# Neighbouring inner channels on one partition: 8192-byte stretches in the experts' down loads, every second column in the transposes

## What is computed

```python
def swiglu(h, w1, w3, w2):
    a = jnp.einsum('bsd,df->bsf', h, w1)
    b = jnp.einsum('bsd,df->bsf', h, w3)
    return jnp.einsum('bsf,fd->bsd', jax.nn.silu(a) * b, w2)

for e in range(N_EXPERTS):                       # 8 experts
    out = out + gates[..., e:e + 1] * swiglu(h, w1[e], w3[e], w2[e])
```

## Time and profile before

| | |
|---|---|
| device time, median of 3 | 1605.03 us (1604.75 to 1606.97) |
| device time of the profiled execution | 1604.42 us |
| its span on the core | 1602.6 us |
| TensorE busy | 1583.4 us (99%) |
| TensorE's weight loads | 1396.0 us (87%), beside the matmuls |
| VectorE busy | 1287.5 us (80%) |
| ScalarE busy | 1042.5 us (65%) |
| read from HBM | 450.74 MB, 282 GB/s over the span |
| expert loads | 336 issues of 1024 KB, 5.4 us to landing (median) |

### The profile page before, as it was taken

One profiled execution on the slowest core, in us unless ns is written; L12 is line 12 of the kernel. 1 busy time (PEld: TensorE's weight loads), 2 busy tenths in 40 slices (PEclk: granted clock), 3 DMA queues, 4 the chain that ended last, 5 costly groups with the idle time before them and its releaser, 6 DMA issues.

```text
span 1602.6 us, 23576 instructions
## 1 busy us (share of the span) xinstructions
PE 1583.4 (99%) x9473; PEld 1396.0 (87%) x9473; DVE 1287.5 (80%) x1137; ACT 1042.5 (65%) x958; POOL 18.7 (1%) x19
## 2 busy tenths in 40 slices
PE   9999999999999999999999999999999999999998
PEld 8999999999999898788888888888888887888886
DVE  6895875445798677998987988897988986988986
ACT  6555554335546557777777776777777776677674
POOL 0000100000000010000000000000000000000000
PEclk9999999999999999999999999999999999999999
DMA  9544545555444456999998999998999998999994
GB/s 298 172 152 139 183 160 185 187 185 191 146 157 159 142 174 227 357 371 359 374 369 325 372 371 360 372 369 311 371 369 362 370 369 308 363 361 378 360 364 173
DMA packets 182503, 453.28 MB, mean 283 GB/s; under 512 B 7168, under 2 KB 81024, under 8 KB 182272
## 3 DMA queue, kind: packets, MB, share of 16 engines
q1 hardware_dynamic: 182400, 451.82, 77.5%
HBM read 450.74 MB, written 1.05 MB: 282 GB/s over the span
## 4 chain that ended last, share of the span: by engine, by line
PE 94%; DVE 3%; ACT 1%; issue 1%; DMA 1%; SPq 0%; ACTq 0%; DVEq 0%
PE bank L310 29%; PE bank L312 29%; PE bank L311 29%; DVE w_low L300 2%; PE bank L1665 2%; PE bank L1643 1%; PE bank L1686 1%; DMA raw<-w_in 1%; ACT w_high L296 1%; PE bank L1283 0%; PE bank L1392 0%; PE bank L1460 0%; PE bank L1343 0%; PE bank L1438 0%; DVE rinv L905 0%
## 5 line engine op out<-in xcount | busy, mean ns | idle before, releaser
L300 DVE TENSOR_TENSOR w_low<-raw,w_high 128x2048 fp32r<-128x2048 f32 x426 | 958.0, 2287 | 124.3 <-ACT w_high L296 124.0
L296 ACT ACTIVATE w_high<-raw 128x2048 fp32r<-128x2048 f32 x426 | 804.2, 1918 | 158.5 <-DMA raw<-exp_w 154.8
L310 PE MATMUL bank<-w_high,hg_high 128*128 128x512 f32 x896 | 352.8, 394 | 4.7 <-DVE w_low L300 3.2
L312 PE MATMUL bank<-w_high,hg_low 128*128 128x512 f32 x896 | 349.7, 390 | 0.0
L311 PE MATMUL bank<-w_low,hg_high 128*128 128x512 f32 x896 | 349.6, 390 | 0.0
L310 PE MATMUL bank<-h_high,w_high 128*128 128x256 f32 x1024 | 290.5, 284 | 0.0
L312 PE MATMUL bank<-h_high,w_low 128*128 128x256 f32 x1024 | 285.7, 279 | 0.0
L311 PE MATMUL bank<-h_low,w_high 128*128 128x256 f32 x1024 | 285.7, 279 | 0.0
L310 PEld LDWEIGHTS bank<-w_high,hg_high 128*128 128x128 f32 x896 | 168.5, 188 | 41.0 <-DVE w_low L300 3.3
L312 PEld LDWEIGHTS bank<-w_high,hg_low 128*128 128x128 f32 x896 | 168.6, 188 | 35.6
L311 PEld LDWEIGHTS bank<-w_low,hg_high 128*128 128x128 f32 x896 | 168.7, 188 | 34.0
(11 more groups left out here) (295 smaller groups left out, 1590.4 us busy)
## 6 DMA issues: line engine op xcount, KB each, us to landing
raw<-exp_w SPq DMA_DIRECT2D x336, 1024.0 KB, 5.4
raw<-w_in SPq DMA_DIRECT2D x41, 1024.0 KB, 5.0
raw<-ffn_w SPq DMA_DIRECT2D x33, 1024.0 KB, 5.1
raw<-w_out SPq DMA_DIRECT2D x8, 1024.0 KB, 4.8
raw<-w_br_attn SPq DMA_DIRECT2D x4, 1024.0 KB, 4.9
raw<-w_br_pool SPq DMA_DIRECT2D x2, 1024.0 KB, 5.2
raw<-w_br_conv SPq DMA_DIRECT2D x2, 1024.0 KB, 4.8
cst<-consts SPq DMA_DIRECT2D x1, 1280.0 KB, 14.1
```

Of the source, the lines that this page charges most:

```text
L296: nc.scalar.activation(wh[c % RING][:], raw[c % RING][:], ACT.Copy).then_inc(s["high_done"], 1)
L300: nc.vector.tensor_tensor(wl[c % RING][:], raw[c % RING][:], wh[c % RING][:].bitcast(F32), ALU.subtract).then_inc(s["split_done"], 1)
L310: pe.matmul(dst, lh, rh, start=start and i == 0, stop=False)
L312: last = pe.matmul(dst, ll, rh, start=False, stop=stop and i == len(terms) - 1)
```

## The change

Partition p of a down piece now takes the neighbouring channels 2p and 2p + 1 of the piece: one stretch of 8192 bytes. To match, block k of the transposes takes every second column (k, k + 2, ...) of 256 columns of `guE`.

```diff
-            e2 = exp_w2[0].rearrange("e (b k p) n -> e b p k n", p=P, k=2)
+            e2 = exp_w2[0].rearrange("e (b p k) n -> e b p k n", p=P, k=2)
...
                 def turn(count, a):
                     pe.wait_ge(s["m_mult"], count + a)
                     for k in range(4):
-                        ins = pe.transpose(bank[TURN_BANKS[a]][:, k * P:k * P + P],
-                                           guE[:, 512 * a + k * P:512 * a + k * P + P], ident)
+                        pairs = guE[:, 512 * a + 256 * (k // 2):512 * a + 256 * (k // 2) + 256].rearrange("p (c two) -> p two c", two=2)
+                        ins = pe.transpose(bank[TURN_BANKS[a]][:, k * P:k * P + P], pairs[:, k % 2, :], ident)
                     ins.then_inc(s["m_t"], 1)
```

## The result

The changed kernel takes 1607.82 us, the median of 20 runs (1604.73 to 1612.65); the kernel before 1604.23 us (20 runs, 1602.10 to 1607.79). The ratio is 1.0024, with a 95% interval from 1.0018 to 1.0031: it is slower by 0.24%, 3.6 us by the medians. (A ratio here is estimated over all executions and is not the quotient of the two medians; in the experiments the two differ by up to 1.3 us.) The time lies in the range that was forecast (1602 to 1611); the forecast of the likeliest case, no change within 0.2%, does not hold to the letter: the measured slowdown stands just beyond that bound, where 0.15 of the chance had been.

The account below looks back on a forecast made before the run. The prediction took TensorE to bound the kernel. From the profiled 1604.42 us, -0.1 for the loads and +0.5 for the transposes gave 1604.8, or 1605.4 us on the scale of the median of runs; range 1602 to 1611.

Parts of the forecast that it names:

- the likeliest case: Whole kernel: loads and transposes both within 1.1 us of nothing, so no change within 0.2%; chance 0.73.
- The bound: Experts' stretch: TensorE, busy 99%, sets the pace of the loads; a load has some 4 us of cover over.
- the 9 us of transfer time: Down loads: 0.08 us saved per piece, 9 us in all; almost none counts on TensorE's path, taken as -0.1 us.
- The packets: Kernel's load queue: 14336 packets fewer, 168064, and that many not under 8 KB beside the 231.
- Their price: Down loads: one packet of 8192 bytes replaces two of 4096 and saves 10 ns of 346, 3%.
- The transposes: 224 weight loads on TensorE, read from `guE` with a step of 8 bytes: +0.5 us in all.
- the near bound: Transposes' weight loads: 1024 bytes passed over at 9.0 bytes per ns, 5 ns more each, 1.1 us in all.
- The nearest row: TensorE's moving operand of 512 columns: 2048 bytes of each partition in 227 ns, 9.0 bytes per ns.
- The bound from above: Transposes' weight loads: each column fetched alone costs twice, 108 ns more each, +24.3 us in all.
- The signs listed for the forecast: New profile: transposes' weight load stays at 138 to 145 ns, four at 0.59 to 0.61 us, a turn at 0.43 us.
- The slower rival: Transposes: strided load halves the rate, load doubles, 1629 us; full chance 0.08, partial over 14 ns per transpose 0.07.
- The 0.80 for "same": Whole kernel: chance of no change, 0.73 for the forecast plus 0.07 for loads that don't become longer packets.

Follow-up runs that it names:

- the loads and the turns alone: Kernel before with only the down loads at 8192 bytes per partition: 1603.76 us, ratio 0.9997; with only the transposes at every second column: 1606.28 us, ratio 1.0018.
- the long row of strided transposes: Kernel before with each turn's transposes made five times over, taking every second column: 1715.05 us, against 1702.72 us for the same with packed transposes.
- the two later measurements: The whole change measured again, unaltered, beside the kernel before: 1608.65 us, ratio 1.0021, and then 1606.53 us, ratio 1.0019.
- the loads alone: Kernel before with only the down loads taking 8192 bytes per partition, transposes packed as before: 1603.76 us, ratio 0.9997.

## Why the prediction came out as it did

**The bound** was read rightly: TensorE sets the pace, and a load has cover. Of the 9 us of transfer time that were to be saved nothing arrives, in the traces (943.3 to 943.4 us against 943.5) or in the times (0.9997, 1.0002, 1.0000 in the three measurements with long packets, packed transposes and a multiply of 684 ns).

**The packets** came as worked out, 168064 and 14336 long ones. Their price came out as well: by the packets' own times in the trace of the changed kernel, from 650 us on, one of 8192 bytes takes 339 ns on average and one of 4096 bytes 175, so the long one saves 10 ns of two short ones, as worked out. In the share of the DMA engines the saving drowns: 78.0% against 77.5% before, and 77.9 and 78.3% with the loads and the turns alone. ScalarE's waits for loads, which might have shrunk by 9 us, did not in this trace (143.0 against 141.9); over the traces of all kernels in the table above they are 137.5 to 144.2 us with long packets and 141.9 to 151.6 without, so a few us may be saved there. None of it reaches TensorE.

**The transposes** are the step that failed in size: "take the middle of 0 and 1.1, +0.5 us". The term measured 224 x 10.4 ns = 2.3 us, twice the upper end of the near bound. The nearest row had been a moving operand that is read packed; it bounded how many bytes are passed over in a time, and said nothing of what a step costs. The bytes that a strided load passes over were the wrong measure, since a step twice as long costs nearly the same. The place was right: the moving operand and the output were left as they were, only the load was made strided, and TensorE paid for each of the 224. The bound from above held too, and so did the 108 ns per packed transpose, which gave 97 us for 896 more of them where 98.7 were measured. The signs listed for the forecast failed too: the load lasts 208 ns, not 138 to 145, and four of them 0.67 us, not 0.59 to 0.61. The slower rival, a load that costs twice, would have gone wrong as well: the load's duration rises by half while its cost on TensorE rises by a tenth (in the long row of strided transposes each load lasts 208 ns and they are 118 ns apart, so the loads overlap).

**The rule of the Trainium skill** ("SBUF — State Buffer", the note on SBUF cachelines). That two hits per line of 16 bytes run at the full rate would have put the sum at 0 for a step of 8 bytes, and a penalty at a step of 16. This case's trace agrees with neither: the load lasts 208 ns, and the transpose costs 10 ns more, at a step of 8; at 16 it is 210 ns and 11 ns more. The measurement decides.

**The rest.** The medians of the whole change stand 3.6, 4.2 and 2.6 us over before, with ratios 1.0024, 1.0021 and 1.0019; the turns explain 2.3 us, 1.0014. The last two intervals hold 1.0014, the first (from 1.0018) does not. The fastest execution of the change is 2.6, 2.4 and 1.8 us above the fastest of the kernel before, near the 2.3, and the table above has 2.9 in its middle. What the medians have beyond that is likely a matter of how often TensorE's clock falls, but this is not shown. One fall like that of the earlier trace rows, which costs 1.6 us, lowers the mean granted clock of an execution by 0.001. The mean over the executions is 0.9972 and 0.9976 for the change in the two later measurements, 0.9977 and 0.9981 for the kernel before beside it: by an estimate from these, half a fall more, 0.8 us. But with the loads alone it was 0.9973 as well, and those were not slower. That the clock falls at the second stop is nothing new: from 1351.0 to 1353.5 us of the changed kernel it was granted 0.50, as in the earlier trace rows, and in the two later profiles of the change it stayed at 1.00 there.

```profile
1351.00:1353.50 2.50, 2.50 (x7) 1.94 (x7) 1.36 (x1) 1.10 (x1) 0.00 (x0) 0.50 0.85 338
```

The line between no change and slower had been drawn at 3.2 us, 14 ns per transpose. With 10 ns the turns alone stay under it, the medians stand around it. The 0.80 for "same" leaned on a bound that no row had tested. That the time lies in the range, 2.4 us above the forecast of 1605.4, is in part luck: the forecast moved by +0.4 us where 3.6 were measured, but it started from a median of three executions that was 0.8 us above that of twenty. The rest is owed to the room that was left above for a dearer load.

## What to carry to other kernels

In this kernel a transfer that was already hidden gained nothing from longer packets, while the rearrangement that pays for them landed on the engine that is the bound. So price the side that pays first, and where no row shows its form, keep the untested bound wide. If data must be re-ordered, try it on another engine, in an operation that it makes anyway; here it was free with the step on the read side and a long inner run, and not with a scattered write. And look at what stands behind that operation on its queue, since an engine that is idle a fifth of the time can still be late at one place. Before two profiles are set against each other, look at the granted clock behind each stop: one fall of it is worth 1.6 us here, over half of what the change costs.

## What the hardware showed that was not expected

- A weight load of 128 float32 columns for a transpose lasts 140 ns packed, 208 ns at a step of 8 bytes and 210 ns at 16; what TensorE pays for one is 108 ns packed and 118 ns at a step of 8 (10.4 ns more by 940 of them in longer rows), and 1 ns more than that at 16, by the sum over all turns.
- VectorE's multiply of 512 elements per partition took 684 ns with both inputs read at a step of two elements, one of them from a bank, as packed; with an inner run of two elements, written 512 bytes apart, it took 1108 ns.
- A stop of TensorE of 1.7 to 2.0 us at the same place of the program was followed by half the granted clock in two profiled executions (1.8 us idle each) and by the full clock in the others (1.68 to 1.96 us idle), so the length of the stop does not tell which comes.
- A packet of 8192 bytes took 339 ns, one of 4096 bytes 175 ns.
